# Two attentions: the query's inverse root moved into the exponential's scale and bias, the rope zeros moved to the key side

## What is computed

```python
q = rms_norm(q.reshape(B, S, N_HEADS, HEAD_DIM), q_norm_w[l])      # first block
k = rms_norm(k.reshape(B, S, N_KV_HEADS, HEAD_DIM), k_norm_w[l])
q = apply_axial_rope(q, ang_r, ang_c)
k = apply_axial_rope(k, ang_r, ang_c)
s = jnp.einsum('bqkgd,bskd->bkgqs', qblk, k) * scale
p = jax.nn.softmax(s, axis=-1)
...
q = rms_norm_2(q, q_norm_g)                                        # second block
k = rms_norm_2(k, k_norm_g)
q = concat([q[..., :128], apply_rope(q[..., 128:], cos, sin)])
k = concat([k[..., :128], apply_rope(k[..., 128:], cos, sin)])     # the rotated part is shared by all heads
```

## Time and profile before

| | |
|---|---|
| median of 3 runs | 3818.86 us (3811.57 to 3819.5) |
| the profiled execution | 3813.55 us, its span 3811.8 us |
| PE busy | 3289.6 us, 86% of the span |
| DVE busy | 2467.6 us, 65% |
| ACT busy | 1440.8 us, 38% |
| first block's attention with its loop, two layers | about 60 to 155 us and 1118 to 1212 us |
| second block's query and key units, two layers | about 2586 to 2666 us and 3408 to 3488 us |

### The profile page before, as it was taken

How to read it: one execution, slowest core, us unless ns; L and a number is a source line. 1 busy time by engine, 2 the same in 40 slices (tenths; PEclk the granted TensorE clock), 3 DMA queues, 4 the chain that set the end, 5 groups by cost and what they waited for, 6 DMA issues and landing times. The chain is left out here.

```text
span 3811.8 us, 50548 instructions
## 1 busy us (share of the span) xinstructions
PE 3289.6 (86%) x18848; PEld 2563.9 (67%) x18848; DVE 2467.6 (65%) x4734; ACT 1440.8 (38%) x2831; POOL 1231.5 (32%) x1160
## 2 busy tenths in 40 slices
PE   5897878877778978788777799999999999999999
PEld 5884433333257943334332499888999998888899
DVE  7775666555667655556566565878666656777665
ACT  3532222222135322212122344565554444555543
POOL 1215777777731147777777300000000000000000
PEclk7998999999998989999999999999999999999999
DMA  7577999999975569999999654433455554333455
GB/s 260 185 259 281 369 360 376 368 355 344 379 287 176 195 257 367 375 362 371 355 344 375 251 183 156 144 122 131 135 164 185 178 183 139 128 127 128 135 185 162
DMA packets 258289, 937.12 MB, mean 246 GB/s; under 512 B 29312, under 2 KB 30720, under 8 KB 257792
## 3 DMA queue, kind: packets, MB, share of 16 engines
q0 software_dynamic: 161280, 587.27, 41.2%
q1 hardware_dynamic: 96768, 346.62, 27.5%
HBM read 932.73 MB, written 1.05 MB: 245 GB/s over the span
## 5 line engine op out<-in xcount | busy, mean ns | idle before, releaser
L635 PE MATMUL M<-rows,diag 128*128 128x512 f32 x2048 | 1001.7, 629 | 332.4 <-DMA rows<-in_expert_v_dram,expert 217.2
L635 PEld LDWEIGHTS M<-rows,diag 128*128 128x128 f32 x2048 | 378.2, 197 | 945.6 <-issue 489.6
L252 DVE TENSOR_TENSOR w_low<-ring,w_high 128x1024 fp32r<-128x1024 f32 x560 | 688.5, 1232 | 402.1 <-ACT w_high L244 398.5
L1093 DVE CUSTOM_DVE_ANT_0 rows<-rows,attn 128x1024 f32<-128x1024 f32 x512 | 610.6, 1223 | 338.0 <-DMA rows<-in_expert_u_dram,expert 336.4
L271 PE MATMUL G<-x_high,w_high 128*128 128x256 f32 x2576 | 765.4, 297 | 57.0 <-DVE w_low L252 23.9
L274 PE MATMUL G<-x_high,w_low 128*128 128x256 f32 x2576 | 738.3, 287 | 0.0
L244 ACT ACTIVATE w_high<-ring 128x1024 fp32r<-128x1024 f32 x560 | 589.3, 1054 | 349.4 <-PE G L271 326.5
L273 PE MATMUL G<-x_low,w_high 128*128 128x256 f32 x2448 | 703.3, 287 | 0.0
L398 POOL DMA_INDIRECT rows<-in_expert_u_dram,expert x512 | 548.0, 1070 | 391.7 <-DVE expert L1075 163.6
L398 POOL DMA_INDIRECT rows<-in_expert_v_dram,expert x512 | 590.5, 1153 | 162.1 <-issue 111.8
L271 PEld LDWEIGHTS G<-x_high,w_high 128*128 128x128 f32 x2576 | 504.6, 196 | 71.5 <-issue 45.8
(11 more groups left out here) (337 smaller groups left out, 4578.8 us busy)
## 6 DMA issues: line engine op xcount, KB each, us to landing
ring<-in_stream_dram SPq DMA_DIRECT2D x654, 512.0 KB, 3.8
ada_ring<-in_ada_stream_dram POOLq DMA_DIRECT2D x80, 512.0 KB, 5.2
rows<-in_ada_stream_dram POOLq DMA_DIRECT2D x16, 512.0 KB, 17.2
rows<-in_expert_u_dram,expert POOLq DMA_INDIRECT x512, 6.4
rows<-in_expert_v_dram,expert POOLq DMA_INDIRECT x512, 6.4
const<-in_const_dram SPq DMA_DIRECT2D x1, 1096.5 KB, 11.5
x<-in_x_dram SPq DMA_DIRECT2D x1, 1024.0 KB, 5.5
out_dram<-x SPq DMA_DIRECT2D x8, 128.0 KB, 3.7
```

The source lines that it names most:

```text
L252: dve.tensor_tensor(T["w_low"][:, part, :], T["ring"][:, place.slot(chunk, slots), :], T["w_high"][:, part, :].bitcast(F32), ALU.subtract) ...
L635: mm = pe.matmul(M[:, 2 * t + half, :], T["diag"][:, n % 4, :], T["v_rows"][:, n % SLOTS, half * 512:(half + 1) * 512], start=(h == 0 and ...
L1093: dve.tensor_tensor_reduce(row, row, T["x_tok"][:, t, :], 1.0, 0.0, ALU.mult, ALU.add, T["hid"][:, r, k:k + 1]).then_inc(sem["u_used"], 1)
```

## The change

In both attentions the query is no longer multiplied by its inverse root. The factor belongs to a token, and in the scores the query's tokens lie on the partitions, so it can be given to the exponential as a scale for each partition, together with the attention's own scale; the maximum is multiplied by it for the bias. For this the root must lie tokens on partitions, 128x2 for each head: PE computes it with the squares as the stationary matrix and one column of ones as the moving one, two matmuls of one column for a query in place of one of 256. The root and the reciprocal are then taken of 128x2. Keys are treated as before in the first block. In the second block the rotated queries are stored once for each pair of heads (`rope_q`), and the zeros are written on the key side, for each of the 8 keys, where before the 8 queries had them.

```diff
# first block, TensorE: unit(u)
-                pe.matmul(NORM[:, 0:S], T["ones_h"][:, :], qsq[:, u % 2, :], start=True, stop=True)
+                if u < KV_HEADS:
+                    pe.matmul(NORM[:, 0:S], T["ones_h"][:, :], qsq[:, u % 2, :], start=True, stop=True)
+                else:
+                    for t in range(TT):
+                        pe.matmul(NORM[:, t:t + 1], qsq[:, u % 2, t * P:(t + 1) * P], T["ones_h"][:, 0:1],
+                                  start=True, stop=True)
                 pe.matmul(NORM[:, S:2 * S], rot, qw[:, u % 2, :], start=True, stop=True
# first block, ScalarE
+            def query_root(h):
+                n = U_NORM + KV_HEADS + h
+                act.wait_ge(sem["norm_full"], n + 1)
+                act.activation(T["qstd"][:, h, :], NORM[:, 0:TT], ACT.Sqrt, bias=T["eps_1"][:, :],
+                               scale=float(HEAD_DIM)).then_inc(sem["std_ready"], 1)
...
                     act.activation(probs[:, h % 2, t, :], SC[:, t * S:(t + 1) * S], ACT.Exp,
-                                   bias=nbias[:, h, t:t + 1], scale=att_scale,
+                                   bias=nbias[:, h, t:t + 1], scale=T["qr"][:, h, t:t + 1],
# first block, VectorE: unit(u)
-                inverse_std(U_NORM + u)
+                if u < KV_HEADS:
+                    inverse_std(U_NORM + u)
                 link(dve.tensor_tensor(rope1[:, :], qw[:, u % 2, :], cos, ALU.mult))
+                dve.wait_ge(sem["std_ready"], U_NORM + u + 1)
                 dve.tensor_tensor(rope2[:, :], NORM[:, S:2 * S], sin, ALU.mult).then_inc(sem["rope_read"], 1)
                 dve.wait_ge(sem["rope_read"], u + 1)
-                link(dve.tensor_tensor(rope1[:, :], rope1[:, :], rope2[:, :], ALU.add))
-                dve.tensor_tensor(qk[:, u, :], rope1[:, :], rstd[:, :], ALU.mult).then_inc(sem["qk_ready"], 1)
+                if u < KV_HEADS:
...
+                else:
+                    dve.tensor_tensor(qk[:, u, :], rope1[:, :], rope2[:, :], ALU.add).then_inc(sem["qk_ready"], 1)
+                    h = u - KV_HEADS
+                    dve.reciprocal(T["qr"][:, h, :], T["qstd"][:, h, :]).then_inc(sem["rstd_ready"], 1)
# first block, VectorE: maxima(h); the second block's softmax(h) changes alike
-                dve.tensor_scalar(nbias[:, h, :], smax[:, h, :], -att_scale, None, ALU.mult
-                                  ).then_inc(sem["bias_ready"], 1)
+                dve.wait_ge(sem["rstd_ready"], U_NORM + KV_HEADS + h + 1)
+                dve.scalar_tensor_tensor(out=nbias[:, h, :], in0=smax[:, h, :], scalar=-1.0, in1=T["qr"][:, h, :],
+                                         op0=ALU.mult, op1=ALU.mult).then_inc(sem["bias_ready"], 1)
# second block, TensorE: unit(u) and softmax(h)
+            if u < MLA_HEADS:
+                for t in range(TT):
+                    mm = pe.matmul(NORM[:, t:t + 1], sq[:, t * P:(t + 1) * P], T["ones_h"][:, 0:1],
+                                   start=True, stop=True)
...
-            pe.wait_ge(sem["qk_ready"], MLA_HEADS + h + 1)
+            pe.wait_ge(sem["qk_ready"], h + 1)
...
-                pe.matmul(out, T["rope"][:, h, q], T["rope_k"][:, h // 2, 0:n], start=False, stop=False)
+                pe.matmul(out, T["rope_q"][:, h // 2, q], T["rope_k"][:, h, 0:n], start=False, stop=False)
# second block, VectorE: unit(u)
-            inverse_std(norm_of["unit"] + u)
...
+            if u < MLA_HEADS:
+                dve.wait_ge(sem["std_ready"], n + 1)
+                dve.reciprocal(T["qr"][:, h, :], T["qstd"][:, h, :]).then_inc(sem["rstd_ready"], 1)
+                return
+            inverse_std(n)
             rows = slice(MLA_ROPE * (h % 2), MLA_ROPE * (h % 2 + 1))
-            if u < MLA_HEADS:
-                other = slice(MLA_ROPE * (1 - h % 2), MLA_ROPE * (2 - h % 2))
-                dve.memset(dst[other, :], 0.0)
+            other = slice(MLA_ROPE * (1 - h % 2), MLA_ROPE * (2 - h % 2))
+            dst = T["rope_k"][:, h, :]
+            link(dve.tensor_tensor(dst[rows, :], T["rope_out"][rows, :], rstd[rows, :], ALU.mult))
+            dve.memset(dst[other, :], 0.0)
             dve.tensor_tensor(T["nope"][:, u, :], T["nope"][:, u, :], rstd[:, :], ALU.mult
```

More of the change, by code:

```diff
@@ L777, in _ @@
                 if i - 1 in unit_at:
-                    root(U_NORM + unit_at[i - 1])
+                    u = unit_at[i - 1]
+                    if u < KV_HEADS:
+                        root(U_NORM + u)
+                    else:
+                        query_root(u - KV_HEADS)
                 if i - 3 in q_at:
@@ L1670, in root, with unit_root @@
                            ).then_inc(sem["std_ready"], 1)
+        def unit_root(u):
+            n = norm_of["unit"] + u
+            if u >= MLA_HEADS:
+                return root(n, P / MLA_QK)
+            act.wait_ge(sem["norm_full"], n + 1)
+            act.activation(T["qstd"][:, u, :], NORM[:, 0:TT], ACT.Sqrt, bias=T["eps_2"][:, :], scale=float(P)
+                           ).then_inc(sem["std_ready"], 1)
         def ffn(g0, g_out, i, beside_out):
@@ L1725, in softmax @@
                 act.activation(T["probs"][:, h % 2, t, 0:n], SC[:, t * S:t * S + n], ACT.Exp,
-                               bias=T["nbias"][:, h, t:t + 1], scale=qk_scale,
+                               bias=T["nbias"][:, h, t:t + 1], scale=T["qr"][:, h, t:t + 1],
                                accum_out=T["rsum"][:, h, t:t + 1]).then_inc(sem["exp_done"], 1)
@@ L1765, in scalar @@
                 "norm_ssd": lambda _: root(norm_of["ssd"], D / SSD_INNER),
-                "unit": lambda u: root(norm_of["unit"] + u, P / MLA_QK),
+                "unit": unit_root,
                 "softmax": softmax, "turn_probs": turn_probs, "values": values,
@@ L2061, in rotate @@
             dve.wait_ge(sem["rope_read"], n + 1)
-            link(dve.tensor_tensor(T["rope_out"][:, j, :], T["rope_in"][:, j, :], T["cos2"][:, :], ALU.mult))
-            link(dve.tensor_tensor(T["rope_out"][:, j, :], T["rope_out"][:, j, :], T["rope2"][:, :],
-                                   ALU.add))
+            out = T["rope_q"][:, j, :] if j < PAIRS else T["rope_out"][:, :]
+            link(dve.tensor_tensor(out, T["rope_in"][:, j, :], T["cos2"][:, :], ALU.mult))
+            link(dve.tensor_tensor(out, out, T["rope2"][:, :], ALU.add))
         def unit_squares(u):
@@ L2075, in unit @@
         def unit(u):
-            inverse_std(norm_of["unit"] + u)
-            h = u % MLA_HEADS
-            rows = slice(MLA_ROPE * (h % 2), MLA_ROPE * (h % 2 + 1))
-            src, dst = ((h // 2, T["rope"][:, h, :]) if u < MLA_HEADS
-                        else (PAIRS, T["rope_k"][:, h // 2, :]))
-            link(dve.tensor_tensor(dst[rows, :], T["rope_out"][rows, src, :], rstd[rows, :], ALU.mult))
-            if u < MLA_HEADS:
-                other = slice(MLA_ROPE * (1 - h % 2), MLA_ROPE * (2 - h % 2))
-                dve.memset(dst[other, :], 0.0)
+            n, h = norm_of["unit"] + u, u % MLA_HEADS
+            if u < MLA_HEADS:
[3 more added lines that the diff above has]
+            inverse_std(n)
+            rows = slice(MLA_ROPE * (h % 2), MLA_ROPE * (h % 2 + 1))
+            other = slice(MLA_ROPE * (1 - h % 2), MLA_ROPE * (2 - h % 2))
+            dst = T["rope_k"][:, h, :]
+            link(dve.tensor_tensor(dst[rows, :], T["rope_out"][rows, :], rstd[rows, :], ALU.mult))
+            dve.memset(dst[other, :], 0.0)
             dve.tensor_tensor(T["nope"][:, u, :], T["nope"][:, u, :], rstd[:, :], ALU.mult
                               ).then_inc(sem["qk_ready"], 1)
-            dve.wait_ge(sem["qk_ready"], u + 1)
+            dve.wait_ge(sem["qk_ready"], h + 1)
         def softmax(h):
@@ L2094, in softmax @@
             link(ins)
-            dve.tensor_scalar(T["nbias"][:, h, :], T["smax"][:, h, :], -qk_scale, None, ALU.mult
-                              ).then_inc(sem["bias_ready"], 1)
+            if h == 0:
+                dve.wait_ge(sem["rstd_ready"], norm_of["unit"] + MLA_HEADS)
+            dve.scalar_tensor_tensor(out=T["nbias"][:, h, :], in0=T["smax"][:, h, :], scalar=-1.0,
+                                     in1=T["qr"][:, h, :], op0=ALU.mult, op1=ALU.mult
+                                     ).then_inc(sem["bias_ready"], 1)
             dve.wait_ge(sem["exp_done"], TT * (h + 1))
@@ L2342, in program @@
                 T1[name] = sb1(name, HEADS, TT)
+            T1["qstd"] = T1["rsum"]
             with ExitStack() as scope_rows:
@@ L2408, in program @@
                 rope = sb2("rope", MLA_HEADS * S)
-                T2["rope"], T2["lora_sq"] = part(rope, 0, MLA_HEADS, S), part(rope, 0, KQ + KC, S)
-                T2["rope_k"] = sb2("rope_k", PAIRS, S)
+                T2["rope_k"], T2["lora_sq"] = part(rope, 0, MLA_HEADS, S), part(rope, 0, KQ + KC, S)
+                T2["rope_q"] = sb2("rope_q", PAIRS, S)
                 y = sb2("y2", 2 * S)
@@ L2430, in program @@
```

(3 more changed lines are left out.)

17 lines of the change are left out of this document (13 added, 4 removed).

## The result

The changed kernel takes 3788.18 us (median of 7 runs, 3772.49 to 3796.76), the kernel before 3817.71 (7 runs beside it, 3811.57 to 3819.5): ratio 0.9914, 95% interval 0.9899 to 0.993, so 33 us less (27 to 39). The ratio is an estimate of its own and not the quotient of the two medians, which is 0.9923, 29.5 us less. The profiled execution took 3777.06 us, 36.5 less than that of before.

A forecast was written before the change was run, and what follows sets the result against it. First block's head steps are bound by ACT and DVE taking turns, with the large reciprocal in the loop; second block nearly by PE. Gains 33.2 + 3.2 = 36.4 us, from 3813.55 or 3818.86 to 3777 or 3782: 3780 us, range 3768 to 3797.

The forecast's parts named there:

- Head steps: First block's attention, five intervals between successive heads' exponentials: each 2.17 us shorter, 10.8 us a layer.
- The priced interval: First block, the one head step priced term by term, exponentials to next exponentials: from 9.46 to 7.29 us.
- Early turns: First block, query-head turns before any exponentials: 6.08 to 4.03 us each, 6.2 to 6.8 us gained a layer.
- Last heads: First block, two intervals and a tail after the query heads: the pointer costs 0.22 us in each, -0.7 a layer.
- Second block: Query units gain 2.8 and 1.58 us, key zeros cost 2.6, last softmax 0.25: 1.6 us gained a layer.
- Sum: Whole kernel: 33.2 us from the first block plus 3.2 from the second, 36.4 us; predicted time 3780 us.
- give-back: Rival, turns behind the attention: weights or adaptive pieces come late, time 3800 to 3812 us; chance 0.05.
- PE as the bound: Rival, first block's head steps: PE limits the interval to 8.5 us, 12 to 14 us less gain, 3793; chance 0.10.
- a clock under 0.8: Sign of being wrong: PE shows waits for the clock's sake in the head steps, granted clock under 0.8.
- the row at 0.64: First block, one step before the change with mean granted clock 0.64 and PE busy 7.98 us; evidence for clock rivals.
- later stages that take longer: Sign of being wrong: the stage from 155 us on takes longer than before.
- Half clock over whole steps: Rival, head steps: PE at 1.2 GHz needs 12.7 us a step, kernel slower at 3844 us; chance 0.04.

The follow-up runs named there:

- run 3: Changed kernel plus an unused 128x256 reciprocal on DVE for each query head of the first block: 3808.2 us, ratio 0.9974 to the kernel before.
- run 1: Kernel before with only the first block's attention changed: 3786.83 us, ratio 0.9918.
- run 2: Kernel before with only the second block's attention changed: 3821.3 us, ratio 0.9999.
- run 8: Kernel before with the first block's query cosine product moved ahead of the wait for the root and the large reciprocal: 3889.66 us, ratio 0.9973.
- run 4: Kernel before with the exponentials' scale read through a pointer, same constant, in both attentions: 3819.86 us, ratio 1.0001.
- run 5: Changed kernel with PE also making the old 256-column norm for each query head of the first block: 3863.91 us, ratio 0.9911 to before.
- the later two: The changed kernel measured twice more, unaltered, beside the kernel before: 3852.57 us, ratio 0.9893, and 3776.55 us, ratio 0.9888.
- run 10: Second measurement of the changed kernel with first-block maxima ahead of the next unit's rotation and second-block zeros in query units: 3768.05 us, ratio 0.9864 to before.
- run 6: Changed kernel with first-block maxima ahead of the next unit's rotation and second-block zeros in query units, first measurement: 3848.89 us, ratio 0.9879 to before.

## Why the prediction was right

The forecast was 3780 with a range of 3768 to 3797 and about 36.4 us of gain. Measured: 3788.18, a gain of 33 (27 to 39), and 36.5 in the profiled pair. That the pair gives the forecast to 0.1 us is luck: by the rows the change is worth 40.8 (below), and stretches that it does not touch lie between. The reason holds: the large reciprocal stood in a loop in which ACT and DVE take turns (run 3), and nearly all of the gain belongs to the first block, 33.2 of 36.4 in the forecast (runs 1 and 2). By its own terms:

- **Head steps**, 10.8 us forecast, 12.1 measured. The priced interval came out at 6.97, not 7.29. The pointer cost less (`w_low` 2.74 us behind the exponentials, not 2.77) and DVE's pitch, the time from one start to the next, is shorter than the 0.46 and 0.19 that I took where the next operation has nothing to wait for: 0.61 for 0.69 behind the division, 0.35 and 0.11 around the small reciprocal. And the other steps gained 2.49 to 2.52 but for the last, 2.12, so that five times the price of one was coarse in any case. The 2.5 us are 1.75 for the reciprocal (run 3), 0.4 for the filled wait (run 8), and, by the rows and with no run of its own, the second product less the small reciprocal, with the shorter pitches, against 0.18 for the pointer (run 4). The 93 ns for a pointer operand in the Trainium skill (ScalarE: Activation LUTs, section "ACT is a hardware spline evaluator") agree with run 4, where the exponential went from 470 to 560 ns; two of them are the 0.18, and I was wrong to prefer 0.11 from other operations.
- **Early turns**, 6.2 to 6.8 forecast. A turn takes 3.83 us (4.03 forecast; its terms add up to 4.02). From the cosine product of the second key to the first exponentials it was 27.2 and 25.9 us, and is 19.2 in both layers: 8.1 and 6.7. The wait of 1.21 us in the first layer is gone altogether, of which I had counted 0.7. But it is not a fixed part of the kernel before: with the same first block the stretch took 25.9 in both layers of run 2 and 27.2 in both of run 4. So this gain is 6.7 to 8.1 a layer, by the execution. "It just fits" for PE was right: at full clock even 0.44 us more cost the two turns 0.01 to 0.03 and the stretch behind them 0.34, and behind a stretch at 0.81 a turn took 0.4 more (run 5).
- **Last heads**, -0.22 each forecast, -0.17 measured (5.87 for 5.70).
- **Second block**, 1.6 us a layer forecast, 1.8 without the last head's softmax; 1.24 from unit 0 to 15. The softmax's 0.25 was not measured apart. Query units with unit 8 gained 4.46 (43.97 to 39.51; I had 2.8 + 1.58), key units lost 3.2, not 2.6: 0.37 in each as priced, and 0.67 more in the first, where the reciprocal stands behind `w_low`. I had not looked at where unit 8's steps stand once the query units before it are short.
- **Sum.** By the rows the change is worth, from the first exponentials to the eighth, 11.8 us in each layer (12.1 less 0.34 for the last two intervals), before them 8.1 + 6.7, and in the second block 2 x 1.24: 40.8 us, 4.4 over the forecast. The first measurement showed 33 (27 to 39), the later two 42 and 43 with wider intervals (24 to 60 and 35 to 51); the medians alone give 29.5, 52.9 and 46.6. I read no give-back out of this: the table shows none, and its scatter is as large as the gap. It is not excluded either: the first measurement by itself leaves 2 to 14 us between its interval and the rows, run 1 likewise (26 to 37 for 38.3 by the rows), and the last none.
- **Rivals and signs.** PE as the bound: excluded for the head steps by run 5, though two of five steps run at a mean clock of 0.74 and 0.76 and PE shows as busy 6.5 us of 6.8. The prediction named a clock under 0.8 in these steps as a sign of being wrong; it came, and the intervals did not move, so it was no sign. Nor was the row at 0.64 a single case: in the kernel before, four of the ten steps stand at 0.64 to 0.81, as long as those at 1.00 (8.97 and 8.98 us, 9.48 and 9.46). The other sign, later stages that take longer, came in one stretch (795.5 for 788.4) and was reversed in the next (839.7 for 845.7), within their scatter. Half clock over whole steps was never seen; but the mechanism exists in small, and in the tighter loop of run 10 it cost 1.5 us a layer.

## What to carry to other kernels

Where two engines take turns, price each operation of the loop as if nothing covered it, then look at what the other engine could already do: here a reciprocal of 128x256 gave back its full 1.75 us, and an order (maxima ahead of the rotation) that nobody needed otherwise was worth another 0.8 us a step on average. A factor that is the same along a row goes into an operand that the next function has anyway; the price is a pointer, 0.09 us for each call. Work that is moved to "somewhere with room" must be placed by who waits behind it: the zeros cost 2.5 us a layer in the key units and nothing in the query units.

## What the runs showed of the hardware

The clock dips for short stretches in a loop in which PE shows as busy nearly all the time. In all six loops of the changed kernel's three profiles the second step had a mean granted clock of 0.74, that is some of the time at 1.2 GHz, and in four of them the fourth had 0.76. With 0.44 us more of matmuls in each unit (run 5, one profile) all ten steps stood at 1.00, and the intervals did not move; in its first layer a dip came ahead of the loop instead (0.81). In a loop with room a dip changes nothing; in one without, as in run 10, it shows as 1.5 us, and PE's scores took 1.91 us for 1.03. The Trainium skill (TensorE: Matmul & The Clock Gate, section "Part 1: The HAM clock gate") has the clock follow how busy PE has been. The steps of run 5 agree with that; runs 6 and 10, the same kernel at 1.00 and at 0.78 in the same step, show that here it does not settle where a dip falls.

Measured prices on 128 partitions: the reciprocal of 256 elements on DVE 1.75 us, four times a product of the same size (0.42); the root of 2 elements on ACT 0.26 against 0.47 for 256; two matmuls of one column 0.50 us, hardly less than the 0.60 of one with 256 columns.
